# An fp32 product of 256 columns into the seventh product's bank, at the opening of each part of the feed-forward layers

## What is computed

```
def _swiglu(x, w_gate, w_up, w_down):
    return (jax.nn.silu(x @ w_gate) * (x @ w_up)) @ w_down
```

## Time and profile before

| | |
|---|---|
| Median of 3 runs | 1614.64 us (1612.23 to 1616.84) |
| The profiled execution's own time | 1613.68 us |
| Its span, first to last instruction | 1611.8 us |
| PE busy | 1598.5 us (99%) |
| DVE, ACT, POOL busy | 1037.2, 794.8, 528.0 us |
| Mean granted TensorE clock | 0.999 |

### The profile page before, as it was taken

One profiled execution on the slowest core, in us unless ns is written; L12 is line 12 of the kernel. 1 busy time (PEld: TensorE's weight loads), 2 busy tenths in 40 slices (PEclk: granted clock), 3 DMA queues, 4 the chain that ended last, 5 costly groups with the idle time before them and its releaser, 6 DMA issues.

```text
span 1611.8 us, 25969 instructions
## 1 busy us (share of the span) xinstructions
PE 1598.5 (99%) x10319; PEld 1438.3 (89%) x10319; DVE 1037.2 (64%) x1470; ACT 794.8 (49%) x1355; POOL 528.0 (33%) x329
## 2 busy tenths in 40 slices
PE   9999999999999999999999999999999999999999
PEld 7989989998888888889899989998768988998998
DVE  5936749567565767556945848657863593674852
ACT  4534536457445455446543536557474353353641
POOL 3150322355563443133150231344333314022132
PEclk9999999999999999999999999999999999999999
DMA  7332333353221445222243343351113223333332
GB/s 204 104 105 86 105 99 107 106 148 85 66 75 57 129 123 154 66 79 79 79 118 92 93 118 105 106 157 46 42 38 79 79 84 113 91 101 110 106 105 79
DMA packets 296066, 157.92 MB, mean 98 GB/s; under 512 B 5265, under 2 KB 292618, under 8 KB 295946
## 3 DMA queue, kind: packets, MB, share of 16 engines
q1 hardware_dynamic: 295946, 156.26, 34.0%
HBM read 154.14 MB, written 2.10 MB: 97 GB/s over the span
## 4 chain that ended last, share of the span: by engine, by line
PE 89%; DVE 6%; ACT 2%; issue 1%; DMA 1%; POOL 0%; SPq 0%; DVEq 0%; POOLq 0%
PE bank L2739 11%; PE bank L2735 11%; PE bank L2736 11%; PE bank L611 9%; PE bank L612 9%; PE bank L615 9%; PE bank L2629 2%; PE bank L2625 2%; PE bank L2626 2%; PE bank L655 2%; PE bank L654 2%; PE bank L659 2%; PE bank L3207 2%; PE bank L634 1%; PE bank L635 1%
## 5 line engine op out<-in xcount | busy, mean ns | idle before, releaser
L519 POOL TENSOR_TENSOR wlo<-wraw,whi 128x1024 fp32r<-128x1024 f32 (+1 forms) x121 | 287.3, 2380 | 368.1 <-ACT whi L514 368.1
L514 ACT CAST whi<-wraw 128x1024 fp32r<-128x1024 f32 (+1 forms) x268 | 274.8, 1029 | 209.7 <-PE bank L615 82.0
L1723 POOL TENSOR_TENSOR hid<-hval,hid 128x512 fp32r<-128x512 f32 x54 | 98.6, 1826 | 527.4 <-ACT hid L1341 527.4
L519 DVE TENSOR_TENSOR wlo<-wraw,whi 128x1024 fp32r<-128x1024 f32 (+1 forms) x147 | 186.7, 1274 | 29.9 <-ACT whi L514 22.8
L1853 DVE SCALAR_TENSOR_TENSOR res<-res,bank 128x512 f32<-128x512 f32 x78 | 52.6, 684 | 215.4 <-PE bank L615 124.1
L611 PE MATMUL bank<-ahi,whi 128*128 128x512 f32 x430 | 171.7, 399 | 0.0
L612 PE MATMUL bank<-alo,whi 128*128 128x512 f32 x430 | 167.7, 390 | 0.0
L611 PE MATMUL bank<-hid,whi 128*128 128x512 f32 x316 | 123.2, 390 | 0.0
L612 PE MATMUL bank<-hid,whi 128*128 128x512 f32 x316 | 123.0, 389 | 0.0
L615 PE MATMUL bank<-ahi,wlo 128*128 128x512 f32 x430 | 107.6, 389 | 0.0
L2735 PE MATMUL bank<-ahi,whi 128*128 128x256 f32 x432 | 106.2, 280 | 0.0
(11 more groups left out here) (433 smaller groups left out, 4226.9 us busy)
## 6 DMA issues: line engine op xcount, KB each, us to landing
wraw<-in_ffn_w_gate SPq DMA_DIRECT2D x42, 512.0 KB, 3.9
wraw<-in_ffn_w_up SPq DMA_DIRECT2D x42, 512.0 KB, 4.6
wraw<-in_ffn_w_down SPq DMA_DIRECT2D x32, 512.0 KB, 4.7
wraw<-in_w_in SPq DMA_DIRECT2D x30, 512.0 KB, 3.8
wraw<-in_w_gate SPq DMA_DIRECT2D x21, 512.0 KB, 3.9
wraw<-in_w_up SPq DMA_DIRECT2D x21, 512.0 KB, 4.4
wraw<-in_w_out SPq DMA_DIRECT2D x16, 512.0 KB, 4.3
wraw<-in_w_down SPq DMA_DIRECT2D x16, 512.0 KB, 4.6
```

The costliest lines, as they stand in the source:

```text
L514: eng.copy(high_of(b)[:, 0:n], raw_of(b)[:, 0:n]).then_inc(hi_ready, 1)
L519: eng.tensor_tensor(low_of(b)[:, 0:n], raw_of(b)[:, 0:n], high_of(b)[:, 0:n], ALU.subtract).then_inc(LO[b][0], 1)
L1723: pool.tensor_tensor(hlo[:, p.m, :], hval[:, p.tile % 2, :], hhi[:, p.m, :], ALU.subtract).then_inc(hidden_ready, 1)
```

## The change

At the opening of each of the nine stretches, ahead of the first quarter product, PE does one more matmul: the fp32 identity by 256 columns of `gate`, the buffer of the tile before, into the bank half of the seventh product. Nobody reads its result: the seventh product starts the same bank half anew. It waits for two signals: that the seventh product of the pair before has been copied away (not in the very first pair), and that the gate of the tile before has been made.

```
+            def spread_start(p):
+
+                if p.n:
+                    pe.wait_ge(*copies.of("seventh", PAIR_LIST[p.n - 1]))
+                pe.wait_ge(gate_done, p.tile)
+                pe.matmul(SEVENTH_BANK, ident, gate[:, (p.tile - 1) % 2, COLS[0]], start=True, stop=True)
+
             def fast_pair(p, opens, nxt):
                 if opens:
+                    spread_start(p)
                     multiply_first(p)
                     multiply_seventh(p)
                     multiply_sixth(p)
```

## The result

The changed kernel takes 1617.67 us in the median of 13 runs (1615.57 to 1618.88), the kernel before 1614.2 us (1612.23 to 1616.84) beside it: a ratio of 1.002, interval 1.0013 to 1.0027. That is 3.5 us more by the medians, 2.1 to 4.4 us by the interval: slower by less than the 0.3% that I called no change, and above my range of 1599 to 1611. It is the number of the first rival, 1617.7, and for this one product the first rival also said what would be seen. The experiments show that its reason does not hold: products of other lengths do move the stream.

A forecast was written before the change was run, and what follows sets the result against it. PE, busy 99% at full clock, was taken to be bound by its instruction spacing. -14.0 at seven openings and +1.4 at one slow waiting opening made -12.6: 1602.0 us, 8-in-10 range 1599 to 1611.

The forecast's parts named there:

- the first rival: Straight behind wide matmuls the spacing does not answer; seven products cost 3.05, the waiting openings nothing: 1617.7 us; chance 0.10.
- What it may give back: Stretches behind the product at 113.3 for 117.8 ns give 1.50, 2.24 or 2.99 us; after price the seven 14.0.
- (b): At the four norms, a slow narrow stream broken by one or two fp32 products goes on fast.
- (d): Wide matmuls, then fp32 turns, then narrow: fast; line 3086 slow at 651.4 us without turns, fast at 671.3 with them.
- (c): At the four norms, a fast narrow stream broken by two or four fp32 products goes on slow.
- rival (3): Only some openings answer: half of the gain, 14 to 7, less 1.4: 1609 us; chance 0.12.
- The price: One fp32 product costs 0.44 us at an opening, hidden by nothing; the seven cost 3.05 us, their waits nothing.
- The two waiting openings: Layers 2 and 3, first stretch: PE waits 1.3 us for silu, loses its stalls; net nothing if the stream stays fast.
- +1.4: One of the two waiting openings taken as slow: 0.27 us up to the former stall and 1.19 behind.
- Rival (4): DVE or ACT can't follow in the three eight-pair stretches, which give nothing back: -7.6 + 1.4, 1608 us; chance 0.04.
- (5): The clock falls to half at the two pauses, 1.6 us each: 1605 us; chance 0.06.
- Rival (2): All openings land slow, slower than before: 7 x 0.44 plus 1.4 for each of two stretches, +5.9, 1620.5 us; chance 0.08.

The follow-up runs named there:

- e2: The change with 254 columns in the fp32 product in place of 256: 1602.08 us, -12.4 to the kernel before.
- e11: The change with one fp32r product of 320 columns in place of the fp32 one, only at the seven openings without a wait: 1598.09 us, -17.0 to the kernel before.
- e8: The change with 256 fp32 columns of constant matrices in place of gate, without the wait for the gate: 1619.69 us, +4.1 to the kernel before.
- e9: The change with one fp32r product of 256 columns in place of the fp32 one, no wait for the gate: 1615.81 us, +0.8 to the kernel before.
- e1: The change with its 256-column fp32 product twice at each of the nine openings: 1606.63 us, -7.8 to the kernel before.
- e4: The change with 128 columns in the fp32 product in place of 256: 1602.09 us, -12.4 to the kernel before.
- e12: The change with 250 columns in the fp32 product in place of 256: 1601.83 us, -12.6 to the kernel before.
- e13: The change with 248 columns in the fp32 product in place of 256: 1618.34 us, +3.9 to the kernel before.
- e3: The change with 252 columns in the fp32 product in place of 256: 1618.05 us, +3.6 to the kernel before.
- e6: The change with 128 columns of gate, only at the seven openings without a wait: 1598.22 us, -17.4 to the kernel before.

## Why the prediction was wrong

**The step that failed** is "What it may give back": that the streams behind the product would run at 113.3 ns. At the seven openings they ran at 117.8, and layer 1's eight pairs took 79.58 us where 76.6 were forecast: the gain of 17 us was nothing, and the price of 3 us was left. I took the gain from (b) and (d) against (c). I had even written that the landing depends on where the stream came from, and did not ask what it depends on in the product. The runs put this in its place: straight behind wide matmuls the length of what stands between decides, to within two columns, and 256 fp32 columns are one of the lengths that leave the stream slow. The rows of (b) had the same product, but a slow narrow stream in front; those of (d) had turns. Neither is this order. My rival (3) gave half of the gain; its counter-argument, the same instructions give one answer, was right, and the answer was "slow" seven times.

**The first rival** has the time, and for this product what was seen, but not the reason. It said that behind wide matmuls the spacing does not answer. It answers to 254 columns, at the same price: e2 took 1602.08 us. That this is the number that I had forecast is partly luck, since both waiting openings are slow in e2's profile, and I had counted one.

**The price** held: 0.44 forecast, 0.43 to 0.44 in each stretch, 3.0 for the seven, and no wait there.

**The size of the gain** held where the spacing answers: 2.53 net forecast for eight pairs, 2.54 in e2. For e2, with the two slow, my steps give -14.0 + 2.8 = -11.2; measured -12.4, the interval -14.7 to -9.8. For e11 they give per layer 1.35 + 2.09 + 2.84 at its price of 0.15, 2.09 + 2.84 per layer 2 and 3, 16.1 in all; measured 17.0, the interval 13.9 to 18.6. Counted in the profiles, the nine stretches together change by what the interval of the run allows, but for two runs: e8's are 5.4 us longer than before, with an interval of 2.3 to 5.3, and e9's 3.2, with 0 to 3.1. In both, layers 2 and 3 are slow in the profile, and e9's profiled execution is the slowest of its ten; why the medians are lower is open.

**The two waiting openings** went nearly as worked out: a wait of 1.25 us (1.3 forecast), the two stalls gone, the end 0.09 late ("nothing"). Both stayed fast, so the +1.4 that I took for one slow opening was not paid; e2 shows that it is the right price, 1.47. Behind the pause the length has a part too, and the other way round: in the seven runs whose two openings wait for the gate (the change, e1 to e4, e12, e13), 12 of the 14 streams there are the opposite of the seven in the same run. With 252 columns and with two products of 256 layers 2 and 3 differ, so something else decides as well; it was not tested.

**Two sums** of the prediction are off, and neither would have changed the range. Rival (4) takes 7.6 us, the net gain of three eight-pair stretches, for what is left; taken off 14.0 it leaves 6.4, which gives 1609.6, or 1611 with the three prices still paid. And 0.27 + 1.19 is 1.46, not 1.4.

**Rivals (4) and (5)** fell: DVE follows in e11, and the clock is at 1.00 behind the pause of 1.25 us. Rival (2) was half seen: its place and price for the seven are right; its two stretches are fast in the change, though slow in e8.

**Shown and open.** Shown: two spacings at one clock; that the product's length picks the one at the seven openings, with either operand and either type; that the spacing accounts for the time within the intervals, e8 and e9 apart. Open: why these lengths. A fixed rhythm of some 6.7 ns (four fp32 columns) would give the alternation of 256 to 248, but as the expectations reckoned with it, it failed for 128 (e4) and for 320 columns (the time that these took), so it is not shown. Open, too, is what picks the spacing behind a pause or a stall.

## What to carry to other kernels

When one instruction form shows two modelled durations at one granted clock, work out the spacing of both stretches: here it was 4.45 ns in 118, and the seven streams' 17 us are 1% of the kernel. Such a stream kept its spacing until something broke it, so look at what stands right in front of it, and try several lengths of a cheap throw-away product there: 254 columns took 12.4 us off where 256 added 3.5, and 320 fp32r columns at the openings that do not wait took off 17.0. A single length that does nothing says little about the idea, and a length that helps in one place can be the wrong one in another: 254 made the seven fast and the two slow.

## What was not expected of the hardware

The same fp32r matmul of 256 columns, with full clock and no idle time, runs at 117.8 or 113.3 ns from start to start, for up to 672 instructions, and two columns in a product ahead of them switch between the two.

PE's idle time of about 2.5 us at 575 was followed by half clock in the profiled execution of the kernel before, and not in the changed kernel's: the last two stages above show it idle for 2.58 us and then 28 matmuls in 3.4 us at 1.00, against 15 at 0.50. Of the fifteen profiles twelve show the half clock there, behind 2.40 to 2.69 us of idle time; the change, e3 and e6 do not, behind 2.58 to 2.60. This is where the changed kernel makes up its delay from layer 1: its first matmul behind the idle time starts 1.33 us later than before (577.80 against 576.47), the one at 579.48 us 0.11 us earlier (579.59 before). It is the main reason why the profiled spans differ by only 1.9 us (1611.8 and 1613.7) where the nine stretches differ by 3.2: a single pair of profiles shows about half of the loss.
